# Prompt attention of a hybrid decoder step: three PSUM banks for scores and two for sums, the addition of halves behind the next scores, and one bias row per forgetting-attention chunk

## The reference

```python
# forgetting attention ("fox"), c = cumsum of log forget gates over tokens
s = q @ k.T * scale + c[query] - c[key];  s = where(key <= query, s, -inf)
o_fox = softmax(s) @ v
# sparse attention: compressed ("cmp"), selected ("slc"; all 16 key blocks here), window of 512 ("win")
s = q @ k.T * scale + rel_bias(query - key);  masked, softmax, @ v
o_nsa = g0 * o_cmp + g1 * o_slc + g2 * o_win
```

## Time and profile before

| | |
|---|---|
| three runs | 1263.92, 1267.36, 1271.39 us; median 1267.36 |
| profiled execution | 1263.59 us, its span from first to last instruction 1261.7 us |
| mean granted TensorE clock | 0.958 |
| busy over the span | TensorE 90%, VectorE 58%, ScalarE 33%, GpSimd 14% |
| prompt attention | from about 530 to 752 us |

### The profile page before, as it was taken

The page is one execution under the profiler, slowest core; times in us unless marked ns, Lnnn a source line. Parts: engine busy times, 40 slices in busy tenths (PEclk is TensorE's granted clock), DMA queues, the critical chain, the costliest instruction groups (busy, mean ns, idle before and its releaser), DMA issues.

```text
span 1261.7 us, 22191 instructions
## 1 busy us (share of the span) xinstructions
PE 1133.6 (90%) x8047; PEld 675.4 (54%) x8047; DVE 735.6 (58%) x1732; ACT 419.0 (33%) x985; POOL 172.2 (14%) x189
## 2 busy tenths in 40 slices
PE   6999999999999999888788889999829999999970
PEld 4676776867866455666565664545423333333320
DVE  6935665855745012578889773436775443344786
ACT  4322524424323010347777771312301110111431
POOL 0122031210311000210000000000000111112243
PEclk9999999999999999979999999999859999999995
DMA  9851030130201303221620007400467978577994
GB/s 288 263 141 31 21 83 3 37 64 20 85 1 52 122 5 63 97 56 29 171 62 2 18 19 211 140 39 17 144 237 258 339 260 291 210 257 255 345 329 160
DMA packets 127320, 164.84 MB, mean 131 GB/s; under 512 B 32257, under 2 KB 101201, under 8 KB 127222
## 3 DMA queue, kind: packets, MB, share of 16 engines
q1 hardware_dynamic: 112070, 109.91, 28.9%
q0 software_dynamic: 15152, 53.60, 11.7%
HBM read 226.35 MB, written 36.47 MB: 208 GB/s over the span
## 4 chain that ended last, share of the span: by engine, by line
PE 75%; DVE 13%; DMA 4%; issue 3%; ACT 2%; SPq 1%; POOL 0%; DVEq 0%; POOLq 0%; ACTq 0%
PE act L743 18%; PE vec L1366 10%; PE vec L778 8%; PE vec L1092 8%; PE vec L753 5%; PE vec L999 4%; PE act L1014 3%; PE vec L794 2%; DVE arena L2107 2%; PE vec L1379 2%; PE act L1379 2%; DMA arena<-x_rows,arena 2%; PE act L1026 2%; DVE arena L2123 1%; PE act L1039 1%
## 5 line engine op out<-in xcount | busy, mean ns | idle before, releaser
L743 PE MATMUL act<-arena 128*128 128x352 f32 x768 | 236.9, 463 | 1.2 <-ACT arena L1460 1.2
L743 PEld LDWEIGHTS act<-arena 128*128 128x128 f32 x768 | 143.1, 190 | 77.6 <-ACT arena L1460 1.7
L1366 PE MATMUL vec<-arena 128*64 128x512 f32 x768 | 172.8, 601 | 1.6 <-DMA arena<-in_exp_w 1.6
L1092 PE MATMUL vec<-arena 128*128 128x512 f32 x256 | 112.9, 594 | 0.8 <-DVE arena L2132 0.8
L1366 PEld LDWEIGHTS vec<-arena 128*64 128x64 f32 x768 | 53.4, 138 | 101.6 <-issue 99.9
L778 PE MATMUL vec<-arena 128*128 128x512 f32 (+1 forms) x256 | 100.3, 546 | 0.0
L1604 ACT COPY arena<-act 128x64 f32<-128x64 f32 (+7 forms) x256 | 70.9, 361 | 50.6 <-PE act L1014 50.5
L1614 ACT ACTIVATE arena<-arena 128x640 f32<-128x640 f32 (+15 forms) x128 | 82.3, 657 | 10.0 <-DVE arena L2107 9.1
L2457 DVE TENSOR_SCALAR arena<-arena 128x256 f32<-128x256 f32 x24 | 7.1, 296 | 129.3 <-ACT arena L1711 129.3
L1092 PEld LDWEIGHTS vec<-arena 128*128 128x128 f32 x256 | 47.4, 189 | 58.2 <-issue 56.8
L2107 DVE CUSTOM_DVE_ANT_0 arena<-vec,arena 128x128 f32<-128x128 f32 (+6 forms) x168 | 68.9, 430 | 16.1 <-PE vec L999 5.8
(11 more groups left out here) (461 smaller groups left out, 1875.3 us busy)
## 6 DMA issues: line engine op xcount, KB each, us to landing
arena<-in_exp_w SPq DMA_DIRECT2D x192, 512.0 KB
arena<-in_exp_w SPq DMA_DIRECT2D x48, 1024.0 KB
y_rows<-arena POOLq DMA_DIRECT2D x24, 512.0 KB, 6.0
arena<-in_w_in SPq DMA_DIRECT2D x16, 512.0 KB, 6.7
arena<-in_x_prompt SPq DMA_DIRECT2D x8, 512.0 KB, 6.4
x_spill<-arena POOLq DMA_DIRECT2D x8, 512.0 KB, 3.2
arena<-x_spill SPq DMA_DIRECT2D x8, 512.0 KB, 5.1
arena<-in_cache_fox_kv SPq DMA_DIRECT2D x16, 256.0 KB, 3.5
```

What stands on the lines that cost most here:

```text
L743: last = mm(bk[:, 0:n], W[k % 2][:, c, m * P:(m + 1) * P], xT[:, c, a:a + n], start=c == 0, stop=c == NC - 1)
L1092: last = mm(bk[:r], src, Wo[half][:, c, :], start=c == 0, stop=c == NC - 1)
L1366: last = mm(gu_bank[p][o], xgT[p][:, c, o], Wgu[:, slot, c, :], start=c == 0, stop=c == NC - 1)
```

## The change

The "vec" banks are divided for the attention: vec 0 to 2 become the ring "score", vec 3 joins act 3 in the ring "summed". The "turned" ring stays act 0 to 2. `add_halves(d)` runs one iteration later, behind the scores of pair d+4 and ahead of `normalise(d+3)`. In place of `cumf` and `foxdiag` each head has two copies of the decay row. Block i uses the copy i % 2, in which GpSimd has added the mask to block i's columns beforehand; when the last fox chunk of block i has been read, GpSimd restores these columns from the other copy. So a fox chunk has one bias row over its whole width. Ahead of the first step on the new ring TensorE waits once until all "vec" banks are drained. The replacement of "vec" by "score" is the same at every step of the stage and is shown once.

```diff
-    banks["turned"], banks["summed"] = banks["act"][0:3], banks["act"][3:4]
+    banks["turned"], banks["summed"] = banks["act"][0:3], [banks["act"][3], banks["vec"][3]]
+    banks["score"] = banks["vec"][0:3]
...
-    cumf, foxdiag = [z.take(1024) for _ in range(2)], [z.take(SEQ, 8) for _ in range(2)]
+    fox_rows = [[z.take(SEQ) for _ in range(2)] for _ in range(2)]
...
         if kind == "fox":
-            off = min(n, i * P - a)
-            whole = [(0, off, cumf[h % 2][:, a:a + off])] if off > 0 else []
-            return whole + ([(n - P, P, foxdiag[h % 2][:, i, :])] if a + n == L else [])
+            return [(0, n, fox_rows[h % 2][i % 2][:, a:a + n])]
...
         def load_decay(h):
-            e.dma_start(cumf[h % 2], bcast(decay_rows[8 * h:8 * h + 8], SEQ)).then_inc(*E.moved(f"cumf{h % 2}_in", ("cumf", h)))
+            for copy in fox_rows[h % 2]:
+                e.dma_start(copy, bcast(decay_rows[8 * h:8 * h + 8], SEQ)).then_inc(*E.moved(f"cumf{h % 2}_in", ("cumf", h)))
...
         E.stage("p3")
+        e.wait_ge(*E.emptied("vec"))
...
-                e.wait_ge(*E.free("vec"))
-                bk = E.bank("vec")
+                e.wait_ge(*E.free("score"))
+                bk = E.bank("score")
...
-                bk = E.banks["summed"][0]
+                bk = E.banks["summed"][E.jobs["summed"] % 2]
...
             if d % 2 == 0:
-                e.wait_ge(*E.at(("foxdiag", h)))
+                e.wait_ge(*E.at(("diagonal masked", h, i)))
+                if i >= 2:
+                    e.wait_ge(*E.at(("row restored", h, i - 2)))
...
+            if it >= 5 and it % 2:
+                add_halves(it - 4)
             if 2 <= it <= n:
                 normalise(it - 1)
-            if it >= 4 and it % 2 == 0:
-                add_halves(it - 3)
+        add_halves(n - 1)
...
+        def mask_diagonal(h, i):
+            row = fox_rows[h % 2][i % 2][:, i * P:(i + 1) * P]
+            tt(row, row, C["diagmask"], ALU.add).then_inc(*E.done(("diagonal masked", h, i)))
+
         for d, (h, i, kinds) in enumerate(PAIRS):
...
-            if d % 16 == 0:
-                if h == 0:
-                    e.wait_ge(*E.at(("cumf", h)))
-                    tt(foxdiag[h % 2], cumf[h % 2].rearrange("p (t k) -> p t k", t=8), C["diagmask"].unsqueeze(1).to_broadcast([P, 8, P]), ALU.add).then_inc(*E.done(("foxdiag", h)))
+            if d == 0:
+                e.wait_ge(*E.at(("cumf", 0)))
+                e.tensor_copy(fox_rows[0][1], fox_rows[0][0]).then_inc(*E.done())
+                e.wait_ge(*E.own())
+                mask_diagonal(0, 0)
+                mask_diagonal(0, 1)
+            if kinds[0] == "fox" and i + 2 < 8:
+                mask_diagonal(h, i + 2)
+                e.wait_ge(*E.at(("scores", d, 0)))
+                used, plain = (fox_rows[h % 2][x][:, i * P:(i + 1) * P] for x in (i % 2, 1 - i % 2))
+                e.tensor_copy(used, plain).then_inc(*E.done(("row restored", h, i)))
             if d % 16 == 9 and h + 1 < H:
                 e.wait_ge(*E.at(("cumf", h + 1)))
-                tt(foxdiag[(h + 1) % 2], cumf[(h + 1) % 2].rearrange("p (t k) -> p t k", t=8), C["diagmask"].unsqueeze(1).to_broadcast([P, 8, P]), ALU.add).then_inc(*E.done(("foxdiag", h + 1)))
+                mask_diagonal(h + 1, 0)
+                mask_diagonal(h + 1, 1)
```

More of the change, by code:

```diff
@@ L966, in decay_sums @@
                 last = mm(bk[:, (t + 1) * H:8 * H], C["negones"], skew(LF[:, t, :], 0, [0, 7 - t], [1, H]), start=False, stop=t == 6)
[L967 removed]
+            last.then_inc(*E.filled("score"))
         def turn_decay_sums():
             e.wait_ge(*E.at("decay sums"))
[L971 to L973 removed]
+            e.wait_ge(*E.free("score"))
+            bk = E.bank("score")
+            e.transpose(bk[0:8 * H, 0:P], decay_cols, ident).then_inc(*E.filled("score"))
         def first_decay_rows(h):
             for g in range(2):
[L977 to L978 removed]
+                e.wait_ge(*E.free("score"))
+                bk = E.bank("score")
                 for c in range(4):
@@ L981, in first_decay_rows @@
                     last = mm(bk[:, c * P:(c + 1) * P], lf, C["negtri"], start=True, stop=True)
-                last.then_inc(*E.filled("vec"))
+                last.then_inc(*E.filled("score"))
         def scores(d):
@@ L995, in scores @@
                     k = {"fox": KT[0:64, h], "slc": KT[64:128, 0], "cmp": KC[64:128]}[kind][:, a:]
-                e.wait_ge(*E.free("vec"))
-                bk = E.bank("vec")
+                e.wait_ge(*E.free("score"))
+                bk = E.bank("score")
                 events = [("queries read", h)] if d % 16 == 15 else []
-                mm(bk[:, 0:n], q[s, h, i * P:(i + 1) * P], k[:, 0:n], start=True, stop=True).then_inc(*E.filled("vec", *events))
+                mm(bk[:, 0:n], q[s, h, i * P:(i + 1) * P], k[:, 0:n], start=True, stop=True).then_inc(*E.filled("score", *events))
         def transposes(d):
@@ L2020, in gelu_inner @@
             x, u = gx[:, o:o + HALF_GELU], gu[:, o:o + HALF_GELU]
-            e.wait_ge(*E.full("vec"))
-            bk = E.job("vec")
+            e.wait_ge(*E.full("score"))
+            bk = E.job("score")
             cp(pc[:, kv:kv + 1], bk[:, 64:65]).then_inc(*E.done())
@@ L2026, in gelu_inner @@
             sampled = skew(bk, 66, [16, DB], [1, NCMPS])
-            ts(x[:, NCMP:].rearrange("p (b n) -> p b n", b=DB), sampled, pc[:, kv:kv + 1], None, ALU.add).then_inc(*E.drained("vec"))
+            ts(x[:, NCMP:].rearrange("p (b n) -> p b n", b=DB), sampled, pc[:, kv:kv + 1], None, ALU.add).then_inc(*E.drained("score"))
             e.wait_ge(*E.own())
@@ L2078, in first_decay_rows @@
                     i = ts(c_[:, n * P:(n + 1) * P], bk[:, c * P:(c + 1) * P], -1.0, carry, ALU.mult, ALU.add)
-                    i.then_inc(*(E.done() if c < 3 else E.drained("vec", ("cumf", h))))
+                    i.then_inc(*(E.done() if c < 3 else E.drained("score", ("cumf", h))))
         def scores(d):
@@ L2109, in scores @@
                     events = [("scores", d, j)] + ([("strips used", h)] if d % 16 == 15 else [])
-                    ins.then_inc(*(E.drained("vec", *events) if x == len(pieces) - 1 else E.done()))
+                    ins.then_inc(*(E.drained("score", *events) if x == len(pieces) - 1 else E.done()))
         def normalise(d):
```

54 lines of the change are left out of this document (24 added, 30 removed).

## The result

| | before | after |
|---|---|---|
| median (runs) | 1267.87 us (13) | 1275.11 us (13) |
| range of the runs | 1262.61 to 1273.24 | 1267.86 to 1279.75 |
| ratio, 95% interval | | 1.0059 [1.0037, 1.0081] |
| profiled execution, span | 1263.59, 1261.7 | 1267.86, 1266.0 |
| mean granted TensorE clock | 0.958 | 0.958 |

The change makes the kernel slower by 7 us (5 to 10). The prediction, 1266 us in a range from 1257 to 1274, is wrong: the median is 1.1 us above the range, and the change is slower where I called it most likely the same. The profiled execution after is the fastest of its 13, so the traces show only 4.3 of the 7 us.

A forecast was written before the change was run, and what follows sets the result against it. It took a prompt-attention loop over VectorE, ScalarE and TensorE as the bound, VectorE nearest full. Terms -2.4 (A) +1.8 (B) -5.0 (C) +5.0 (D) +1.5 (E) made +0.9 us; it named 1266 us, range 1257 to 1274.

The forecast's parts named there:

- B: Fourth score chunk at i of 4 or more, three score banks: product waits for VectorE, delaying transposes and exponentials; +1.8 us.
- the sum: All priced terms of the prompt attention together: +0.9 us on the profiled 1263.59 us, with 1266 us named as the time.
- rival 3: Fourth chunk at i = 4 to 7, 16 times: third score bank too few, +10 in all, 1275 us; chance 0.13.
- the 1.22 in the text: Pair at i=7: transposes begin near T+1.22 us, T being VectorE's start of the pair, 0.70 us later than before.
- the slacks: ScalarE's exponentials ready before VectorE asks: 0.25 us at i=7, 0.61 at i=6, 1.00 at i=4.
- A: Fox chunks with whole blocks and diagonal: one VectorE bias instruction for two, 0.26 us each; -2.4 us counted, at i = 1 to 3.
- C: Four bulk mask additions on GpSimd go, and with them stalls of VectorE's small instructions: 5.0 us gained.
- D: 56 small GpSimd masks and restores come and lengthen VectorE's normalisation instructions at i = 1 to 4: +5.0 us, bounds 0 and 10.
- E: Start of the attention: the three-bank ring delays decay sums, their turning and the second compression product; +1.5 us, bounds 0 and +4.
- F: Halves added behind the next scores, two banks of sums: the wait at heads' ends only moves, nothing gained; zero.

The follow-up runs named there:

- the fourth product later: Changed kernel, but TensorE issues the fourth score product of a fox and slc pair behind the first group of transposes: 1258.27 us, ratio 0.9944 to before.
- rows alone: Kernel before with only the bias rows changed (two decay-row copies, small GpSimd masks and restores), four score banks, one of sums: 1256.37 us, ratio 0.9908 to before.
- banks alone: Kernel before with only the banks changed (three for scores, two for sums), old bias rows and place of the halves: 1285.14 us, ratio 1.0135 to before.

## Why the prediction was wrong

**B failed, and with it the sum.** I named the place and the mechanism, and rival 3 named the cause, but I gave that rival 0.13. Two steps went wrong.

The first is the term "the fourth product needs 0.46 (a quarter of TensorE's 1.8 us for four)". Products run in twos there, and the fourth, late and alone, took 0.96 us. (Of the 1.22 in the text 0.07 had no source: 0.69 and 0.46 make 1.15.) So the transposes were 1.18 us late at i=7, not 0.70, and by the same way of reckoning the slacks do not hold. At i=7 it is 1.18 - 0.25 = 0.93 us. At i=6 it is 1.18 - 0.61 = 0.57. At i=5, where the transposes came 1.08 us later and ScalarE's next copy stood 0.95 us ahead of the normalisation in head 2, it is 0.13, and at i=4 the slack of 1.00 covers 0.87. In four heads that is an estimate of 6.5 us for a B of 1.8, and of +5.6 for the sum: 1271 in place of 1266.

The second is "the transposes [...] on which ScalarE's copies and then the exponentials of pair d wait": I followed one branch of what stands behind the fourth product. The other is TensorE's own program: second transposes, value sums, next scores. Before, the win scores at i=7 started at T+3.22 and VectorE came to them at T+4.76; with the fourth product later it takes them at T+4.07 without a wait. So they had some 0.7 us of slack, and A and the moved addition (0.26 and 0.28) brought VectorE earlier by most of that. Being first in VectorE's program, this wait covers that for the exponentials: 0.87, 1.20 and 1.10 us at i = 5, 6 and 7 for scores, and then 0.17 at i=7 for exponentials. The small 0.5 us in the table of waits is therefore no sign that ScalarE had slack.

The twelve win steps grew by 14.3 us. B as I defined it is net of A: fox and win steps of i = 5 to 7 grew by 9.1 us together, 10.5 without the stall in head 1 that C had booked, against +1.8. Of that some 6.5 is the mis-sized delay by the estimate above, and the rest the branch left out. Rival 3's time, 1275, met the measured one, but that is luck in part: it told of 16 waits for exponentials, and the runs show twelve waits for scores.

**A** was right in mechanism and price, 0.26 us a chunk. I let B eat it at i = 5 to 7, but the steps of fox 5, 6 and 7 in head 2 are 0.40, 0.30 and 0.38 us shorter than before: the loss is in another step, and both count. The rows alone show it whole: 9.4 us of stretch against the same kernel with two instructions, some 6 of them A and the rest the spells of lower clock.

**C** was about right. The stalls named are gone: fox i=4 in head 0 from 4.39 to 3.42 us (0.97, as booked), in head 1 the steps of win 4 and fox 5 from 10.30 to 6.87 (3.4; booked 3.56 from i=4 to i=5). The copy of 1024 columns took 1.05 us, the lower bound.

**D** was half of what I took. The mask took 0.45 us against my 0.3 (and the 0.28 of the estimate beside it), the restore 0.29, yet only the tail met VectorE: the steps of win i=2, 3 and 4 in head 2 are 0.21, 0.08 and 0.39 us longer, i=1 not at all. That is 0.7 a head, 2.7 in all, against 5.0. Two masks for the next head at i=4 are most of it, as said; i=1 was counted 0.4 for nothing.
The Trainium skill ("SBUF — State Buffer", Who interferes with whom) has the two engines take a shared port pair in turn. The trace agrees in both directions: L2120 took 0.39 us beside a mask for 0.16 alone, and a mask took 0.69 beside L2126 for 0.45 alone.

**E** was about right: with the banks alone the first four steps are 1.45 us longer than before (15.90 for 14.45), against 1.5; after, they are 1.0 longer. They are 3.0 longer than with the rows alone, but 2.0 of that is the step of i=3 in head 0, ahead of which the granted clock was 0.97 over 558 to 561 us with the rows alone and 0.50 after. The decay sums are late by 0.82 us (3.07 for 2.25), as read.

**F**: the head's end came as written; the wait of 2.2 us now stands at the scores (the longest of L2110). "Elsewhere the addition only changes its place" was wrong where the bank of sums is single, by 34 us, and holds only because the same change brings the second bank.

**The sum.** With C and E as booked, A at i = 5 to 7 too (12 x 0.26 = 3.1), D at 2.7 and the win steps' 14.3 in place of B it is -2.4 - 3.1 + 14.3 - 5.0 + 2.7 + 1.5 = +8.0, where the stretch grew by 5.1. Of the rest 0.7 is A at i = 1 to 3 without the part I took off, 0.5 the start, and 1.4 a step of fox i=3 in head 3 that was 3.94 us before without an addition on GpSimd beside it, and 2.29 after.

## What to carry to other kernels

When an instruction gets a new wait, list everything behind it in its engine's own program, up to the next product that another engine asks for, and not only its direct consumers; price the wait at the consumer with the least slack, which here was the next pair's first score at i = 5 and 6, with the exponentials close behind. Measure a job's cost alone before it is moved out of a stream: a quarter of the time of four was half of what the fourth took by itself. When a ring gets shorter than a burst that uses it, move the burst's last job behind work that needs none of its banks: that returned 13.5 of the 14.3 us. And price a resource together with what frees it: the later addition cost 34 us with one bank of sums and nothing like that with two.

## What the runs showed that I had not expected

- Score products run in twos: three took 1.98 us and four 1.99. The fourth, kept back for its bank, took 0.96 us by itself and held the transposes back by 1.18 us. Kept back behind the transposes it costs almost nothing: the steps of i = 4 to 7 sum to 110.95 us with three banks and 110.8 with four.
- Where TensorE is late its granted clock falls in some heads and not in others with the same program: with the banks alone it was 0.50 over 624 to 634 us, the lower level of 1.2 GHz. What decides it is open.
- Merging 24 pairs of instructions, 6 us of VectorE's time, took 9.4 us off the stage between two traces: one has three such spells and the other none. That the merging keeps the clock up is not shown.
